# Output and query copies ahead of the exponentials in the mixers of a four-layer backbone

## The reference

```python
for i in range(DEPTH):                      # DEPTH = 4
    kind, j = i % N_MIXERS, i // N_MIXERS   # A, B, C, D
    xp = half_ffn(xp, mp[0], mp[1], mp[2], norm_ff1[i], ff1_w_gu[i], ff1_w_down[i])
    hp = modulate(xp, norm_mix[i], mp[3], mp[4])
    # A: 16 heads on 4 key heads, window, sink logit;  B: the same, global, with rotary
    # C: queries and keys/values from compressed latents (ranks 384 and 256)
    # D: 16 heads, neighbourhood attention with a learned bias
    q, k, v = gqa_project(hp, a_w_qkv[j], a_q_norm[j], a_k_norm[j], A_HEADS, A_KV_HEADS)
    op = merge_heads(block_attention(group_q(q, A_KV_HEADS), k, v, a_sink[j]), a_w_o[j])
    xp = xp + mp[5] * op
    xp = half_ffn(xp, mp[6], mp[7], mp[8], norm_ff2[i], ff2_w_gu[i], ff2_w_down[i])
```

## Time and profile before

| | |
|---|---|
| median of 3 runs | 2980.02 us (2980.00 to 2980.03) |
| profiled execution | 2978.57 us, its span 2976.7 us |
| PE busy | 2906.3 us |
| DVE busy | 2288.0 us |
| ACT busy | 1246.5 us |
| mixers A, B, C, D start at | 318, 1031, 1738, 2492 us |
| and end (next stage's norm) at | 480, 1187, 1941, 2700 us |

### The profile page before, as it was taken

How to read it: one execution, slowest core, us unless ns; L and a number is a source line. 1 busy time by engine, 2 the same in 40 slices (tenths; PEclk the granted TensorE clock), 3 DMA queues, 4 the chain that set the end, 5 groups by cost and what they waited for, 6 DMA issues and landing times.

```text
span 2976.7 us, 44338 instructions
## 1 busy us (share of the span) xinstructions
PE 2906.3 (98%) x17575; PEld 2811.6 (94%) x17575; DVE 2288.0 (77%) x3506; ACT 1246.5 (42%) x2001; POOL 127.6 (4%) x135
## 2 busy tenths in 40 slices
PE   8999989999999998999999999999999999999999
PEld 6999879999999988999999987799999999889999
DVE  6889887888788877788888867678888877667653
ACT  3332464443333355443333247644333323554432
POOL 0000110000000010000000011000000001320000
PEclk9999999999999999999999999999999999999999
DMA  7556304555455511555455521155545555314332
GB/s 286 205 215 229 120 31 161 187 211 201 178 190 197 201 67 66 197 190 208 186 187 193 215 98 52 57 194 188 202 188 190 190 220 175 107 60 183 127 137 96
DMA packets 87721, 490.21 MB, mean 165 GB/s; under 512 B 11824, under 2 KB 13168, under 8 KB 51376
## 3 DMA queue, kind: packets, MB, share of 16 engines
q1 hardware_dynamic: 83696, 480.42, 43.5%
q0 software_dynamic: 3904, 8.24, 1.1%
HBM read 485.33 MB, written 3.29 MB: 164 GB/s over the span
## 4 chain that ended last, share of the span: by engine, by line
PE 54%; issue 37%; DVE 4%; ACT 3%; DMA 1%; POOL 0%; SPq 0%; DVEq 0%; ACTq 0%; POOLq 0%
PE ps L748 16%; PE ps L767 8%; PE ps L753 8%; PE ps L788 6%; PE ps L943 4%; PE ps L771 4%; PE ps L732 1%; PE ps L887 1%; DMA boot<-in_mod_w 1%; PE ps L922 1%; PE ps L872 1%; PE ps L865 1%; PE ps L961 0%; DVE C_stat L1774 0%; ACT w_hi L1127 0%
## 5 line engine op out<-in xcount | busy, mean ns | idle before, releaser
L748 PE MATMUL ps<-h_hi,w_hi 128*128 128x386 f32 x2688 | 908.5, 338 | 0.0
L748 PE MATMUL ps<-h_lo,w_hi 128*128 128x386 f32 x2688 | 893.4, 332 | 0.0
L1444 DVE TENSOR_TENSOR w_lo<-w_raw,w_hi 128x2048 fp32r<-128x2048 f32 (+3 forms) x282 | 705.8, 2503 | 40.6 <-ACT w_hi L1127 40.2
L1464 DVE CUSTOM_DVE_ANT_0 F_junk<-F_slab,cond,mod_b 128x1024 f32<-128x1024 f32 x544 | 706.4, 1299 | 12.7
L1127 ACT ACTIVATE w_hi<-w_raw 128x2048 fp32r<-128x2048 f32 (+4 forms) x278 | 578.7, 2082 | 17.7 <-DMA w_raw<-in_ffn_dn 11.5
L748 PEld LDWEIGHTS ps<-h_lo,w_hi 128*128 128x128 f32 x2688 | 512.6, 191 | 0.0
L748 PEld LDWEIGHTS ps<-h_hi,w_hi 128*128 128x128 f32 x2688 | 503.1, 187 | 0.3 <-ACT w_hi L1127 0.3
L753 PE MATMUL ps<-h_hi,w_lo 128*128 128x386 f32 x2688 | 494.3, 335 | 0.0
L767 PE MATMUL ps<-F_act_hi,w_hi 128*128 128x384 f32 x1408 | 473.8, 336 | 0.0
L767 PE MATMUL ps<-F_act_lo,w_hi 128*128 128x384 f32 x1408 | 473.4, 336 | 0.0
L753 PEld LDWEIGHTS ps<-h_hi,w_lo 128*128 128x128 f32 x2688 | 468.9, 187 | 0.0
(11 more groups left out here) (358 smaller groups left out, 3320.2 us busy)
## 6 DMA issues: line engine op xcount, KB each, us to landing
w_raw<-in_ffn_gu SPq DMA_DIRECT2D x176, 1024.0 KB, 4.7
F_slab<-in_mod_w SPq DMA_DIRECT2D x272, 512.0 KB, 5.6
w_raw<-in_ffn_dn SPq DMA_DIRECT2D x64, 1408.0 KB, 6.4
w_raw<-in_d_w SPq DMA_DIRECT2D x8, 1536.0 KB, 6.9
boot<-in_mod_w SPq DMA_DIRECT2D x8, 1024.0 KB, 10.2
w_raw<-in_a_w SPq DMA_DIRECT2D x4, 1536.0 KB, 6.6
w_raw<-in_b_w SPq DMA_DIRECT2D x4, 1536.0 KB, 6.4
w_raw<-in_c_w SPq DMA_DIRECT2D x8, 544.0 KB, 3.6
```

Of the source, the lines that this page charges most:

```text
L748: pe.matmul(ps[:, 2 * par + u, 0:N_MOVE], w[0][:, k, u, :], h[:, k, :], start=(k == 0 and h is h_hi), stop=False)
L1444: dve.tensor_tensor(w_lo[par][:, 0:w], w_raw[par][:, 0:w], w_hi[par][:, 0:w], ALU.subtract).then_inc(w_split_lo.sem, 1)
L1464: dve.tensor_tensor_reduce(out=junk[:], in0=w, in1=cond[:, c, :], scale=scale, scalar=mod_b[:, n:n + 1], op0=ALU.mult, op1=ALU.add, accum_ ...
```

## The change

Five edits of order, all in the mixers:

1. A, B, D: the first turn of queries and keys stands ahead of the last six matmuls of the second group's projection. To make room, the second group's tiles use banks 7, 6, 3 and not 7, 6, 5, and `scores(1)` takes over the wait for their copies.
2. ScalarE, all mixers: `o_hi` stands right behind `p_copy`, ahead of the exponentials and, in C and D, of `raw`. In A and B the copies of queries and keys stand ahead of the exponentials too.
3. VectorE: `o_lo` stands right behind `inverse`. In C and D the head sums of the last group (pass 12) move behind both.
4. C: where a projection tile ends an odd pass, the queries are turned, then the tile, then the keys.
5. Three unused pieces of SBUF (24, 48, 8 words) shift what lies behind them by 96, 288 or 32 bytes; the output tiles start 32 bytes off a multiple of 64 where they started on one.

```diff
-def proj_bank(g, t):
-    return (t, B_P - t, B_P)[min(g, 2)]
+def proj_bank(kind, g, t):
+    return (t, B_P - t if kind == "C" else (B_P, B_O, B_WARM)[t % 3], B_P)[min(g, 2)]
...
+                    part("space_cq", [P, 24])
...
+                    part("space_o", [P, 48])
...
+                    part("space_o", [P, 8])
...
-            def turn_qk(s, p):
+            def turn_qk(s, p, half=None):
...
-                pe.wait_ge(qn_ready.sem, qn_ready.after((s, g)))
-                if p == 0:
+                if half != 1:
+                    pe.wait_ge(qn_ready.sem, qn_ready.after((s, g)))
+                if p == 0 and kind == "C":
...
                 for i, (what, n, w) in enumerate(qkt_types(kind, p)):
+                    if half is not None and i // 2 != half:
+                        continue
...
                 if b >= 2:
                     pe.wait_ge(exp_ready.sem, exp_ready.at[(s, p, x)] - 1)
+                elif b == 1:
+                    pe.wait_ge(raw_ready.sem, raw_ready.after((s, 1), proj_tiles(kind) - 1))
...
-                    for t in range(proj_tiles(kind)):
+                    for t in range(TT - 1):
                         projection(s, 1, t)
+                    projection(s, 1, TT - 1, 0, KD - 2)
                 turn_qk(s, 0)
+                if kind != "C":
+                    projection(s, 1, TT - 1, KD - 2, KD)
...
-                    if b % 2 == 1 and b + 1 < BATCHES:
-                        turn_qk(s, (b + 1) // 2)
-                    for piece in fills(kind, b):
-                        if piece[-1]:
-                            projection(s, *piece)
+                    turn = (b + 1) // 2 if b % 2 == 1 and b + 1 < BATCHES else None
+                    late = [piece for piece in fills(kind, b) if piece[-1]]
+                    halves = kind == "C" and turn is not None and late
+                    if turn is not None:
+                        turn_qk(s, turn, 0 if halves else None)
+                    for piece in late:
+                        projection(s, *piece)
+                    if halves:
+                        turn_qk(s, turn, 1)
...
                     if 2 <= b < BATCHES + 2:
                         p_copy(s, b - 2)
+                    if b >= 4 and b % 2 == 0:
+                        o_hi(s, b // 2 - 2)
...
                     if kind in "AB":
                         for g, t in done[0]:
                             raw(s, g, t)
+                        if b % 2 == 1 and b + 1 < BATCHES:
+                            qk_copies(s, (b + 1) // 2)
...
-                    if b >= 4 and b % 2 == 0:
-                        o_hi(s, b // 2 - 2)
-                    if b % 2 == 1 and b + 1 < BATCHES:
+                    if kind in "CD" and b % 2 == 1 and b + 1 < BATCHES:
                         qk_copies(s, (b + 1) // 2)
...
+                    sums_first = per == 1 and g + 2 < n_g
...
-                        if i == 0:
+                        if i == 0 and sums_first:
                             head_sums(s, g + 1)
-                        elif kind == "C":
+                        elif i == 1 and kind == "C":
                             scale_heads(s, g + 1)
                     if 1 <= b < BATCHES + 1:
                         inverse(s, b - 1)
+                    if b >= 4 and b % 2 == 0:
+                        o_lo(s, b // 2 - 2)
                     if norm_next:
+                        if per == 1 and i == 0 and not sums_first:
+                            head_sums(s, g + 1)
...
-                    if b >= 4 and b % 2 == 0:
-                        o_lo(s, b // 2 - 2)
```

More of the change, by code:

```diff
@@ L787, in project @@
                     for i, (x1, x2) in enumerate(((h_hi, 0), (h_hi, 1), (h_lo, 0))):
-                        mm = pe.matmul(ps[:, proj_bank(g, t), 0:QKV_W], x1[:, k, t * P:(t + 1) * P],
+                        mm = pe.matmul(ps[:, proj_bank(kind, g, t), 0:QKV_W], x1[:, k, t * P:(t + 1) * P],
                                        rh[x2][par][:, k * QKV_W:(k + 1) * QKV_W],
@@ L1015, in up @@
                     for i, (x1, x2) in enumerate(((0, 0), (0, 1), (1, 0))):
-                        mm = pe.matmul(ps[:, proj_bank(g, t), col:col + w], lh[x1][:, k, t * P:(t + 1) * P],
+                        mm = pe.matmul(ps[:, proj_bank("C", g, t), col:col + w], lh[x1][:, k, t * P:(t + 1) * P],
                                        rh[x2][par][:, at + k * w:at + (k + 1) * w],
@@ L1197, in raw @@
                     act.wait_ge(kv_out, kv_sent[s, g - 4])
-                bank = ps[:, proj_bank(g, t), :]
+                bank = ps[:, proj_bank(kind, g, t), :]
                 if kind != "C":
@@ L1324, in compress @@
                     ins = act.activation(v["sq0"][:, t].rearrange("p h d -> p (h d)"),
-                                         ps[:, proj_bank(0, t), 0:C_UQ_W], ACT.Square)
+                                         ps[:, proj_bank("C", 0, t), 0:C_UQ_W], ACT.Square)
                 ins.then_inc(c_q_sq_ready, 1)
@@ L1332, in raw_queries @@
                 return act.activation(v["qraw"][g % 2][:, t].rearrange("p h d -> p (h d)"),
-                                      ps[:, proj_bank(g, t), 0:C_UQ_W], ACT.Copy)
+                                      ps[:, proj_bank("C", g, t), 0:C_UQ_W], ACT.Copy)
             def squares():
```

## The result

| | before | after |
|---|---|---|
| median (9 runs each) | 2980.02 us (2977.57 to 2981.31) | 2987.62 us (2984.71 to 2990.11) |
| ratio | | 1.0025, 95% interval 1.0015 to 1.0035 |
| profiled execution | 2978.57 us, span 2976.7 | 2988.55 us, span 2986.7 |
| mixer A, B, C, D, us | 161.9, 155.6, 203.1, 208.3 | 157.6, 152.3, 212.5, 216.8 |

The change makes the kernel slower by 7.6 us. The forecast was 2987.0. A mixer's length is counted from its own norm to the next stage's. The feed-forward stages are equal to within 0.1 us each (0.2 to 0.3 us shorter in all), so the change lies in the mixers: -4.3, -3.3, +9.4 and +8.5 us.

A forecast was written before the change was run, and what follows sets the result against it. TensorE, busy 2906.3 us of a 2976.7 us span, was taken to bound the kernel. The terms 16.7 - 9.5 + 1.2 - 1.6 + 0.2 gave +7.0 us, a forecast of 2987.0 us, range 2978 to 2994 us.

The forecast's parts named there:

- second tile behind the raw copy: All mixers, passes still projecting: TensorE's second projection tile waits for ScalarE's raw copy, queued behind `o_hi`; +16.7 us together.
- low parts and copies: Mixers A, B, C: TensorE's waits for low parts of outputs and for query and key copies shrink; -9.5 us together.
- key turn in C: Mixer C, six odd passes: the tile's matmuls between queries and keys put the keys 0.2 us later; +1.2 us.
- given back in C: Mixer C, odd passes: VectorE gains 0.5 us on TensorE, so waits for scaled keys shrink; -1.6 us.
- pass 12 and D's tail: Mixers C and D: later head sums delay the next maximum, in D nearly paid by a low-part wait; +0.2 and +0.1 us.
- starts of A, B, D: Mixer starts: transposes leave the chain, the last six matmuls enter it, copies stay behind the last raw copy; -0.1 us.
- half-clock stretches: TensorE at 1.2 GHz: one stretch may go in A, one may come in C's pass 13; nothing, 3 us as bounds.
- Where nothing can be won, a wait adds its full length: Mixers C and D, passes 4 to 11: TensorE is busy 18.90 of 18.90 us, so added waits count in full.
- The gains: Mixers A, B, C: waits that go with early output copies and low parts, less what VectorE gives back; -9.5 us.
- The rival in which it sets the pace further out: Mixer tails: VectorE sets the pace, so half of the 9.5 us comes back; +11.8 us, 2991.8 us; chance 16%.
- The 32 bytes: Output tiles' shifted start: 6 ns by 768 output matmuls, 4.6 us either way, taken as nothing; part of a 16% rival.
- Each new wait drops the clock: Mixers C and D: eight half-clock stretches of 1.65 us each; +20.2 us, 3000.2 us; chance 6%.

The follow-up runs named there:

- experiments 1: The changed kernel with output copy and low part back in their old places in passes that still project; 2970.21 us, ratio to before 0.9966.
- experiment 9: The changed kernel with the output copy right behind the raw copy, ahead of the latent exponentials, in passes that still project; 2971.18 us, ratio 0.9968.
- experiment 2: The kernel before with only the output copy moved early, in mixer D's passes 4 to 10; 2988.76 us, ratio 1.0028.
- experiment 5: The changed kernel with mixer C's queries and keys turned in one piece ahead of the late tile, as before; 2986.97 us, ratio 1.0022.
- experiment 4: The changed kernel with four filler matmuls in each of the eight second-tile waits of mixers C and D; 2986.37 us, ratio 1.0022.

## Why the prediction was right

The forecast was right in its main mechanism, and in time in part by luck: its sum was some 2 us too high, and the clock, which it took as nothing, made that good. Term by term, from the passes of the profiled executions (us):

| step | forecast | measured |
|---|---|---|
| second tile behind the raw copy, A and B | 1.04 each | 1.05 each |
| the same in C, four times | 1.91 each | 1.88 to 1.89 each (experiments 1, 9) |
| the same in D, four times | 1.74 each | 1.74 to 1.75 each (experiments 1, 2, 9) |
| low parts and copies, A | -4.1 | -4.3 |
| the same, B | -4.7 | -4.7 |
| the same, C | -0.7 | -1.1 |
| key turn in C, six | 0.2 each | 0.15 to 0.18 each (experiment 5) |
| given back in C | -1.6 | -1.7 (0.46 three times, 0.3) |
| pass 12 and D's tail | 0.3 | -1.0 |
| starts of A, B, D | -0.1 | 0.29, 0.31, -0.14: +0.5 |
| half-clock stretches | 0 | +5.2 |
| span | +7.0 | +10.0 |

The measured rows add up to 10.5, the mixers themselves to 10.3; the feed-forward stages are 0.2 to 0.3 shorter.

- *Where nothing can be won, a wait adds its full length.* This is the step that decided, and it held to 0.03 us each time. It needed no rule beyond: 18.90 of 18.90 us. The chain was the right one, and ScalarE passed nothing in its queue: 4.33 us idle in front of a waiting copy.
- *The gains.* VectorE gives back part of what goes in A (its waits for scaled probabilities grow from 4.4 to 5.9 us), as priced. The rival in which it sets the pace further out falls: half of 9.5 did not come back.
- *Pass 12 and D's tail* was mis-sized. The chain is as written: VectorE waits 2.41 us for the power, and TensorE's turn comes no later against the maxima than before (6.5 us behind the end of pass 12's, 6.6 before). But the late maximum cost 0.6 us and not 1.2, and TensorE gained 1.2 in pass 15 and 0.4 at the drain, where I had 1.1. Without the clock D is 5.8 us longer where I had 7.1.
- *The starts* were mis-sized the other way: I saw that the copies stay behind the last raw copy, and still booked a small gain. They cost 0.3 in A and in B.
- *The 32 bytes* were taken as nothing, with 4.6 us either way as the rival. In the two kernels without the shift (before and experiment 2) output products that follow one another without a wait start 175.6 and 175.2 ns apart on average, in all ten with it 173.5 to 173.6. That is 2 ns, by an estimate from 768 products about 1.5 us of gain, and no run has the shift alone. The rival falls as put; this gain stands inside the measured rows of the passes with output products.
- *The clock.* I took it as nothing on balance, with 3 us as bounds. In the profiled execution it is +5.2 us: stretches came at 1775 (2.3), 1891 (1.5), 2635 (1.5), and 2659 had twice the length of the one before (1.2), while the one at 437 went (-1.3). Without it the change is +4.8 us of span, where I had 7.0. By the runs at equal clock the change costs 5.9 to 7.3 us and the medians differ by 7.6, so the clock's share in the medians lies between 0.3 us (by the runs) and 2.8 us (by the passes). The good agreement of 2987.0 with 2987.6 is in part this accident.
- *Each new wait drops the clock* falls as put, with its 20 us, but has a part in it: six in 36 do (experiment 4), and the change also joined waits into longer ones, 4.2 us in C's pass 13, where the longest had been 1.5, and 3.3 in D's for 2.3. Both had a stretch at their end or behind it in all seven profiles that have them. With the shorter waits of the sums first it was so in three of five profiles in each mixer, so the longer wait may bring the stretch more often; that the two are linked is not shown otherwise. I had counted the lengths of waits and not what a longer one brings with it.

Open is why a half-clock stretch follows a wait of one length in one run and not in the next, and what the shift of the output tiles is worth by itself.

## What to carry to other kernels

Before an instruction that waits is moved forward in a queue, list what then stands behind it and who waits for that; here a copy of 0.5 us held up a copy on which the saturated engine's next tile hung, and cost 1.7 us each time. Make the move only in the passes where no such copy stands behind it: ahead of the raw copy it cost 7 us in four passes of one mixer, just behind the raw copy it cost nothing (experiment 9), and in the late passes of two others it was part of a group of moves that gained 4 to 5 us in each. When work is moved on one engine, move its consumers on the next engine in the same edit.

## What the runs showed of the hardware that was not expected

- A program's own runs differ by up to 8.8 us (2976.7 to 2985.5 of the kernel before) in step with the mean granted clock of 0.999 to 0.994. At one level of that clock (known to 0.001) the runs still lie up to 3.2 us apart (2977.1 to 2980.3 at 0.998). Comparing pass by pass tells 0.2 us where medians of nine runs tell some 3.
- What TensorE did before the clock fell: in the mixers of the twelve profiles it stood idle for over 1.9 us in one piece 33 times, and 31 times the clock was at half within 2.5 us of the end of it. These are three places of the program (one in A, and one each in pass 13 of C and D), so they are not 33 separate cases. Of 148 idle times of 1.0 to 1.9 us, 18 had the same; the same wait of 1.3 us at the start of C had 6.8 us at half behind it in four profiles (2.3 us more) and none in eight. A stretch of 3.4 us cost 1.5 us where TensorE was busy through it, and less where it waited for others.
